# Expert weights laid with consecutive rows in a partition, and the feature order that follows

## The reference: what is computed

```python
def rms_norm(x, g):
    xf = x.astype(jnp.float32)
    y = xf * lax.rsqrt(jnp.mean(xf * xf, axis=-1, keepdims=True) + RMS_EPS)
    return (y * g.astype(jnp.float32)).astype(x.dtype)
...
    x = x + merged @ w_mix_o[l]
    h = rms_norm(x, norm_ffn_g[l])
    x = x + hierarchical_moe(h, ...)          # router: 36 logits a token, 2 of 32 experts chosen
...
def expert_block(args):                       # xb: the rows routed to expert e
    xb, e = args
    hid = jax.nn.silu(xb @ w_gate[e]) * (xb @ w_up[e])     # 1024 -> 512
    return hid @ w_down[e]                                 # 512 -> 1024
```

## Time and profile before

| | |
|---|---|
| time, median of 3 runs | 2509.94 us (2508.97 to 2510.35) |
| span of the profiled execution (first to last instruction) | 2510.5 us |
| TensorE busy | 2324.1 us, 93% |
| VectorE, ScalarE, GpSimd busy | 1099.5, 455.0, 121.8 us |
| bytes moved by DMA | 483.90 MB in 178413 packets |
| mean granted TensorE clock | 0.969 of full |

### The profile page before, as it was taken

The page is one execution under the profiler, slowest core; times in us unless marked ns, Lnnn a source line. Parts: engine busy times, 40 slices in busy tenths (PEclk is TensorE's granted clock), DMA queues, the critical chain, the costliest instruction groups (busy, mean ns, idle before and its releaser), DMA issues. The chain is left out here.

```text
span 2510.5 us, 29002 instructions
## 1 busy us (share of the span) xinstructions
PE 2324.1 (93%) x11012; PEld 1343.9 (54%) x11013; DVE 1099.5 (44%) x1871; ACT 455.0 (18%) x854; POOL 121.8 (5%) x53
## 2 busy tenths in 40 slices
PE   5999999996999999999789999999969999999995
PEld 2448888543455455455344588885435455455453
DVE  6895334324333433433378843434243433433433
ACT  2103333001111111111121223320001111111111
POOL 0002212000000000000000022210000000000000
PEclk9999999998999999999979999999979999999997
DMA  5201101232698898898241011121329898898891
GB/s 191 76 17 51 68 34 68 101 140 101 251 351 329 320 353 325 323 354 325 78 183 42 34 51 51 51 78 74 140 101 335 323 346 333 321 348 330 323 350 42
DMA packets 178413, 483.90 MB, mean 193 GB/s; under 512 B 4128, under 2 KB 4896, under 8 KB 172960
## 3 DMA queue, kind: packets, MB, share of 16 engines
q1 hardware_dynamic: 178336, 482.88, 52.0%
HBM read 476.57 MB, written 6.29 MB: 192 GB/s over the span
## 5 line engine op out<-in xcount | busy, mean ns | idle before, releaser
L754 PEld LDWEIGHTS ps<-arena 128*128 128x128 f32 x2176 | 249.9, 195 | 43.0 <-issue 26.0
L754 PE MATMUL ps<-arena 128*128 128x128 f32 x2176 | 256.4, 280 | 16.4 <-DVE arena L285 16.4
L1612 PE MATMUL ps<-arena 128*64 128x512 f32 x512 | 252.4, 605 | 3.2 <-DVE arena L1357 3.2
L1613 PE MATMUL ps<-arena 128*64 128x512 f32 x512 | 252.4, 605 | 0.0
L1353 DVE TENSOR_TENSOR x_tokens<-x_tokens,ps 128x512 f32<-128x512 f32 x272 | 181.2, 686 | 146.6 <-PE ps L748 145.4
L1612 PE MATMUL ps<-slabs,arena 128*64 128x512 f32 x512 | 225.0, 592 | 0.0
L1613 PE MATMUL ps<-slabs,arena 128*64 128x512 f32 x512 | 224.9, 592 | 0.0
L1346 DVE SCALAR_TENSOR_TENSOR split_rows<-ps,arena,split_rows 64x512 fp32r<-64x512 f32 x128 | 96.0, 750 | 276.4 <-ACT split_rows L957 274.4
L573 PE MATMUL ps<-h_hi,w_parts 128*128 128x512 f32 x768 | 211.6, 411 | 0.0
L428 PE MATMUL ps<-slabs,hT 128*128 128x512 f32 x384 | 174.5, 616 | 9.1 <-DVE hT L1254 7.5
L573 PEld LDWEIGHTS ps<-h_hi,w_parts 128*128 128x128 f32 x768 | 141.5, 194 | 25.7
(11 more groups left out here) (280 smaller groups left out, 3012.3 us busy)
## 6 DMA issues: line engine op xcount, KB each, us to landing
arena<-in_expert_w_gate SPq DMA_DIRECT2D x32, 2048.0 KB, 8.7
arena<-in_expert_w_up SPq DMA_DIRECT2D x32, 2048.0 KB, 13.6
arena<-in_expert_w_down SPq DMA_DIRECT2D x32, 2048.0 KB, 11.1
slabs<-in_expert_w_gate SPq DMA_DIRECT2D x32, 2048.0 KB, 9.7
slabs<-in_expert_w_up SPq DMA_DIRECT2D x32, 2048.0 KB, 14.5
slabs<-in_expert_w_down SPq DMA_DIRECT2D x32, 2048.0 KB, 8.2
slabs<-in_dense SPq DMA_DIRECT2D x18, 2048.0 KB, 8.5
slabs<-in_gate_w SPq DMA_DIRECT2D x24, 1024.0 KB, 4.8
```

What stands on the lines that cost most here:

```text
L754: last = nc.tensor.matmul(ps[:, 2 + d // 4, (d % 4) * P:(d % 4 + 1) * P], xn[:, t, d * P:(d + 1) * P], sel[:, t, :], start=(t == 0), stop= ...
L1612: nc.tensor.matmul(ps[0:64, bank, :], x_k, wg_k, start=(k == 0), stop=(k == ND - 1), tile_position=(0, 0))
L1613: return nc.tensor.matmul(ps[64:P, bank, :], x_k, wu_k, start=(k == 0), stop=(k == ND - 1), tile_position=(0, 64))
```

## The change

The expert weights are laid so that partition `p` takes consecutive rows: rows `8p` to `8p+7` of gate and up, `4p` to `4p+3` of down. A partition's share of a matrix is then one run of 16 KB. Features must lie in the same order in everything that meets these weights:

- `normalise` of the second norm (k = 1) reads x with a step of 8 features and writes `xn` in the order chunk, partition;
- `gffn` and the router's weights `rw` are loaded again in that order, by eight DMAs each of 16 partitions (and one DMA for the router's bias `rb`); the source of the former is single 4-byte elements;
- `hid` is written in the order chunk, partition: the reads stay consecutive, and each written element lies 128 elements (512 bytes) behind the last. 

`w_place` is each slot as a flat run of 4096 elements; the matmuls read it through the same views as before.

```diff
+        w_place = [[view(o, SLAB) for o in w] for w in wslot]
+        def by_rows(a):
+            return a.rearrange("q (c p) -> q p c", c=NH)
+        def in_fours(a):
+            return a.rearrange("q (p c) -> q p c", c=NH)
...
             def expert_rows(ap, e, k):
-                return ap[bass.ds(layer, 1), bass.ds(e, 1)].rearrange("l e (k p) n -> p (l e k) n", p=P, k=k)
+                return ap[bass.ds(layer, 1), bass.ds(e, 1)].rearrange("l e (p k) n -> p (l e k n)", p=P, k=k)
...
                             sp.dma_start(io["x_kept"].rearrange("(t p) d -> p t d", p=P), x).then_inc(s["x_saved"], 16)
+                            sp.wait_ge(s["small_in"], 16)
+                            a0 = SMALL["gffn"][0]
+                            for j in range(ND):
+                                sp.dma_start(small["gffn"][16 * j:16 * j + 16, :],
+                                             row(io["small"])[:, a0 + j].rearrange("(a k) -> a k", k=ND),
+                                             allow_slow_non_contiguous=True).then_inc(s["gffn_in"], 16)
...
-                    sp.dma_start(view(O_KS + N_MCONST, 324), row(io["router"])).then_inc(s["router_in"], 16)
+                    for j in range(ND):
+                        sp.dma_start(rw[16 * j:16 * j + 16], row(io["router"])[:, 36 * j:36 * j + 36].rearrange("(a k) n -> a k n", k=ND))\
+                          .then_inc(s["router_in"], 16)
+                    sp.dma_start(rb, row(io["router"])[:, 288:324]).then_inc(s["router_in"], 16)
...
-                            sp.dma_start(w_gate[b], expert_rows(io["expert_w_gate"], e, ND)).then_inc(w_in_sem[b][0], 16)
+                            sp.dma_start(w_place[b][0], expert_rows(io["expert_w_gate"], e, ND)).then_inc(w_in_sem[b][0], 16)
...
-                    pe.wait_ge(s["router_in"], 16)
+                    pe.wait_ge(s["router_in"], 16 * (ND + 1))
...
-                        tell(v.tensor_scalar(xn[:, t, :], x[:, t, :], rstd[:, one], None, ALU.mult), "xn_ready")
+                        to, of = xn[:, t, :], x[:, t, :]
+                        if k == 1:
+                            to = to.rearrange("q (k p) -> q k p", k=ND)
+                            of = of.rearrange("q (p k) -> q k p", k=ND)
+                        tell(v.tensor_scalar(to, of, rstd[:, one], None, ALU.mult), "xn_ready")
...
                     dve.wait_ge(s["x_back"], 16)
+                    dve.wait_ge(s["gffn_in"], 16 * ND)
...
-                                v.tensor_tensor(hid[0:64], ps[64:P, 0, :], silu[0:64], ALU.mult).then_inc(s["hid_done"], 1)
+                                v.tensor_tensor(by_rows(hid[0:64]), in_fours(ps[64:P, 0, :]), in_fours(silu[0:64]), ALU.mult)\
+                                 .then_inc(s["hid_done"], 1)
```

More of the change, by code:

```diff
@@ L323, in _ @@
                 act.wait_ge(s["pro_act"], 2)
-        names = ("small_in", "bparam_in", "sgu_in", "cglu_in", "router_in", "mconst_in", "slab_in0", "slab_in1", "slab_in2",
+        names = ("small_in", "gffn_in", "bparam_in", "sgu_in", "cglu_in", "router_in", "mconst_in", "slab_in0", "slab_in1", "slab_in2",
                  "chain_dve", "chain_act", "chain_pool", "sumsq_ready", "var_ready", "sd_ready", "xn_ready",
@@ L389, in _ @@
                     sp.wait_ge(s["merge_done"], ND)
-                    load_expert(nc, sp, io, expert_rows, 0, 0, w_gate, w_up, w_down, w_in_sem)
+                    load_expert(nc, sp, io, expert_rows, 0, 0, w_place, w_in_sem)
                     sp.wait_ge(s["outp_done"], ND)
-                    sp.dma_start(view(O_KS + N_MCONST, 324), row(io["router"])).then_inc(s["router_in"], 16)
+                    for j in range(ND):
+                        sp.dma_start(rw[16 * j:16 * j + 16], row(io["router"])[:, 36 * j:36 * j + 36].rearrange("(a k) n -> a k n", k=ND))\
+                          .then_inc(s["router_in"], 16)
+                    sp.dma_start(rb, row(io["router"])[:, 288:324]).then_inc(s["router_in"], 16)
                     sp.dma_start(mc, io["mconsts"]).then_inc(s["mconst_in"], 16)
                     sp.wait_ge(s["proj_done"], J_END - 4)
-                    load_expert(nc, sp, io, expert_rows, 1, 1, w_gate, w_up, w_down, w_in_sem)
+                    load_expert(nc, sp, io, expert_rows, 1, 1, w_place, w_in_sem)
                     with sp.Fori(0, N_EXP // 2 - 1) as i:
@@ L400, in _ @@
                             sp.wait_ge(s["gu_done"], 2 * i + b + 1 + CRED)
-                            sp.dma_start(w_gate[b], expert_rows(io["expert_w_gate"], e, ND)).then_inc(w_in_sem[b][0], 16)
-                            sp.dma_start(w_up[b], expert_rows(io["expert_w_up"], e, ND)).then_inc(w_in_sem[b][1], 16)
+                            sp.dma_start(w_place[b][0], expert_rows(io["expert_w_gate"], e, ND)).then_inc(w_in_sem[b][0], 16)
+                            sp.dma_start(w_place[b][1], expert_rows(io["expert_w_up"], e, ND)).then_inc(w_in_sem[b][1], 16)
                             sp.wait_ge(s["down_done"], 2 * i + b + 1 + CRED)
-                            sp.dma_start(w_down[b], expert_rows(io["expert_w_down"], e, NH)).then_inc(w_in_sem[b][2], 16)
+                            sp.dma_start(w_place[b][2], expert_rows(io["expert_w_down"], e, NH)).then_inc(w_in_sem[b][2], 16)
                 @block.tensor
@@ L1276, in _ @@
                     dve.wait_ge(s["rt_done"], 1)
-                    dve.wait_ge(s["router_in"], 16)
+                    dve.wait_ge(s["router_in"], 16 * (ND + 1))
                     dve.wait_ge(s["mconst_in"], 16)
@@ L1464, in _ @@
                                 def _(sp):
-                                    for w, name, k in ((w_gate, "expert_w_gate", ND), (w_up, "expert_w_up", ND),
-                                                       (w_down, "expert_w_down", NH)):
-                                        sp.dma_start(w[0], expert_rows(io[name], e, k)).then_inc(so["ov_weights"], 16)
+                                    for w, name, k in zip(w_place[0], ("expert_w_gate", "expert_w_up", "expert_w_down"), (ND, ND, NH)):
+                                        sp.dma_start(w, expert_rows(io[name], e, k)).then_inc(so["ov_weights"], 16)
                                     sp.wait_ge(so["ov_weights"], 48)
@@ L1526, in _ @@
                                     dve.wait_ge(so["ov_silu"], 1)
-                                    v.tensor_tensor(hid[0:CAP], ps[64:P, 0, :], silu[0:CAP], ALU.mult).then_inc(so["ov_hid"], 1)
+                                    v.tensor_tensor(by_rows(hid[0:CAP]), in_fours(ps[64:P, 0, :]), in_fours(silu[0:CAP]), ALU.mult)\
+                                     .then_inc(so["ov_hid"], 1)
                                     for n in range(2 * NT):
@@ L1592, in reduce_angle, with load_expert @@
     link(v.tensor_scalar(r2, r2, -1.0, float(np.pi / 2), ALU.mult, ALU.add))
[L1595 to L1598, removed]
+def load_expert(nc, sp, io, expert_rows, e, b, w_place, w_sem):
+    sp.dma_start(w_place[b][0], expert_rows(io["expert_w_gate"], e, ND)).then_inc(w_sem[b][0], 16)
+    sp.dma_start(w_place[b][1], expert_rows(io["expert_w_up"], e, ND)).then_inc(w_sem[b][1], 16)
+    sp.dma_start(w_place[b][2], expert_rows(io["expert_w_down"], e, NH)).then_inc(w_sem[b][2], 16)
 def expert_gather(nc, ps, bank, xn, sel):
```

## The result

| | before | after |
|---|---|---|
| median of 4 runs of each | 2509.45 us (2505.15 to 2510.35) | 2519.85 us (2518.04 to 2521.90) |
| span of the profiled execution | 2510.5 us | 2520.1 us |
| VectorE busy | 1099.5 us | 1126.4 us |
| mean granted TensorE clock of that execution | 0.969 | 0.970 |

The ratio is 1.0046, with a 95% interval of 1.0034 to 1.0057, that is 8.5 to 14.3 us more; the medians differ by 10.4 us and the profiled spans by 9.6 us. The forecast was 7.2 us more. The changed kernel's profiled execution was the slowest of its four (2521.9 us of device time beside a span of 2520.1), so places in the two traces are compared by their lengths, not by their totals.

What follows compares the result with a forecast made beforehand. The prediction took TensorE to bound the kernel, with weights always arriving in time. hid's 6.4 us and the norm's 0.8 gave +7.2 us, loads 0: 2509.9 + 7.2 = 2517.1 us, range 2509.2 to 2524.

Steps and rivals of the forecast that it cites:

- The bound, and the loads: Expert loop: TensorE bounds it, weights always arrive before they are asked for, so larger packets are worth 0 us.
- Rival (d): Expert loads: long runs are slower and loads bound the loop; 15% longer loads give +57 us; chance 0.04.
- (e): Expert loads: 16 KB runs are cut into 2 KB packets, packets stay near 178,000, time as forecast; chance 0.40 together with forecast.
- Rival (c): First products: fewer DMA packets relieve TensorE's reads, 6.7 us come back, 2503.2 us with a free hid; chance 0.05.
- The cover of 0.17 us: Each pair's first expert: spare time per pair before a longer hid on VectorE stops TensorE's transposes.
- rival (a): Stepped write: it is free, or hid grows by less than 0.3 us; 2510 to 2514 us; chance 0.33.
- (b): Each hid element takes two cycles (+11.8 us), norm between 0.8 and 3.2; 2523.2 us; chance 0.18.
- the term of 6.4: hid in the expert loop: 0.37 us longer, 0.17 covered, so 0.20 us per pair, 32 times, 6.4 us.
- The prediction's upper bound: hid's stepped write: one element in two cycles in place of one adds 0.54 us, 11.8 us in all.
- The norm: Each layer's fourth second-norm instruction: its read step costs 0.42 us, 0.8 us in two layers.
- The small loads: gffn's eight and the router's nine DMAs on SyncE: hidden by spare time, all 0 us.
- The baseline: Profiled span of 2510.5 us, taken as 0.6 us above the runs' median; forecast carried to the median from 2509.9.

Runs made afterwards that it cites:

- e1: Kernel before with only the experts' weights laid in 16 KB runs, so the experts' products differ in value: 2508.12 us, 1.000 times before.
- e7: Kernel before with only w_down laid in long runs and hid written with the 512-byte step: 2515.08 us, 1.0024 times before.
- e12: Changed kernel, gffn and router weights reordered in HBM beforehand, hid in two instructions, first two transposes awaiting only the first: 2509.55 us, 1.0000 times before.
- e8: Changed kernel, gffn and router weights reordered in HBM beforehand, hid written consecutively with both inputs read in 16-byte steps: 2517.11 us, 1.0032 times before.
- e11: Kernel before, with half of each layer's last norm computed twice, without a step: 2511.52 us, 1.0008 times before.
- e6: Changed kernel, gffn and router weights reordered in HBM beforehand, w_down and hid as before the change: 2511.32 us, 1.0009 times before.
- e9: Changed kernel, gffn and router weights reordered in HBM beforehand, 49 counting instructions per layer added on SyncE: 2518.15 us, 1.0037 times before.
- e3: Changed kernel with hid written consecutively and its transposes on TensorE reading every fourth element: 2604.22 us, 1.0379 times before.
- e5: The changed kernel measured again, with nothing else altered: 2520.03 us, 1.0040 times before.
- e10: Changed kernel with gffn laid out in HBM beforehand, so only the router's nine small DMAs remain: 2517.92 us, 1.0037 times before.
- e2: Kernel of e1 with hid also written in the 512-byte step; tokens went to other experts: 2859.99 us, 1.1397 times before.

## Why the prediction held, and what it missed

**The bound, and the loads: right.** e1's packets (39072 for 178336) are worth 0 within 2.8 us. Rival (d) falls with the same run, and (e) with 43763 packets, against about 43,750 forecast (8992 under 512 bytes, against 8,990). Rival (c) supposed that many packets slow the first products on `arena`. With a quarter of them the page after has

```profile
L1637 PE MATMUL ps<-arena 128*64 128x512 f32 x512 | 252.3, 605 | 3.2 <-DVE arena L1381 3.2
...
L1638 PE MATMUL ps<-slabs,arena 128*64 128x512 f32 x512 | 224.9, 592 | 0.0
```

the same 605 and 592 ns as the earlier trace rows. The 13 ns have another cause, which stays open.

**hid: right in mechanism and size.** The row taken as nearest, the 16-byte step of line 1315 with 0.73 ns more per element, gave 0.37 us; (1069 - 693)/512 = 0.73 ns and 0.376 us were measured. The cover of 0.17 us came out as 0.376 - 0.20 = 0.18. That excludes rival (a), a free step, and (b), whose 0.54 us more would have made `hid` 1.23 us. e7 puts 6.1 us (3.8 to 8.3) on the term of 6.4, and e12 shows that it is the stall that counts and not VectorE's time. The Trainium skill, "SBUF — State Buffer", section "Door 1: The DMA port swizzle", says that each access to a new 16-byte line pays a penalty; it gives no size for it. e8 and the change agree with it: steps of 16 bytes on the reads and of 512 on the write cost the same, 376 ns for 512 elements. No run here has a step below 16 bytes. The prediction's upper bound, said there to be the sum by this rule, rests on a doubling that is the prediction's own, and the runs show 0.70 of it (376 of 540 ns).

**The norm: right in length, open beyond it.** 0.39 us per layer against 0.42. The prediction scaled line 1585 by 0.52 ns per element; e11 bears that out with 0.49 us for 512 elements beside 0.75 for 1024, 0.51 ns each. What the whole costs, e6 gives only as 2.3 us (0 to 4.5).

**The small loads: this step failed, in part.** "All 0 us" holds for their transfers and their issue. SyncE issues `gffn`'s in 14.04 us and the router's in 5.85 and 8.25 us:

```profile
20.91 14.04 SPq L396 DMA_DIRECT2D arena<-in_small  x8
35.14 1.72 SPq L388 DMA_DIRECT2D slabs<-in_dense  x1
...
529.02 0.33 SPq L1621 DMA_DIRECT2D arena<-in_expert_w_gate  x1
529.45 0.38 SPq L1622 DMA_DIRECT2D arena<-in_expert_w_up  x1
529.92 0.43 SPq L1623 DMA_DIRECT2D arena<-in_expert_w_down  x1
530.53 5.85 SPq L408 DMA_DIRECT2D arena<-in_router  x8
536.57 8.25 SPq L410 DMA_DIRECT2D arena<-in_router  x1
```

Slab 2 is issued at 35.14 and needed at 78, and no engine waits. But I had counted the DMAs and their packets, and not the instructions (some 49, the number that e9 puts in their place) that wait, address and issue in SyncE's loop. They delay SyncE's return in the turn between the layers by some 3.1 to 3.9 us: 12.40 to 13.21 us in the five traces that have such code (after, e3, e5, e9, e10), against 9.26 to 9.40 in the nine without it (before and all others). What TensorE pays is less, because ScalarE is no earlier. Its first product on a slab comes 29.5 to 30.0 us behind the `add_back` in the five and 28.3 to 29.0 in the eight others read for it (all but e2), about 1.1 us more in the mean, and the program's end is some 0.5 us longer (23.3 to 23.6 for 22.8 to 22.9; e1, without the code, has 23.4). So the term put at 0 was 1 to 2 us.

The 9.6 us between the profiled spans are then: 5.9 for the intervals between pairs, 0.8 for the norm, 1.3 for the turn and the end, 0.3 net from stretches at another clock, and 1.3 in stretches in which nobody waits for what was changed. The first three, and 0.4 for the two pairs that lie in other rows of the table, are what the change does: 8.4 us, against 7.2 forecast and an interval of 8.5 to 14.3. The parts measured alone by their medians, 6.1 (e7) and 2.3 (e6), leave the remainder open within their intervals of some 2 us each. Why the median came out at 10.4 and not near 8.4 no run here shows; the interval of e5 (7.0 to 13.0) holds both.

The signs were there: the page counts q14's packets, and the turn of 9.26 us stood in the trace. SyncE shows no work in it; the kernel has it clear the layer's semaphores there, between two barriers of all engines. The Trainium skill, "Runtime: NRT & Kernel Launch", section "Instruction fetch mechanics", has the rule that I should have weighed: instructions are fetched in blocks over a DMA queue of their own, in sequence, and a taken branch to outside the window stalls. The loop over the layers is such a branch. The trace agrees as far as it goes. Between the last `add_back` and SyncE's first DMA, q14 moves 2 packets before (1247 to 1256 us) and 6 after (1251 to 1263.6 us):

```profile
q14 instruction: 2, 0.02, 0.6%
...
q14 instruction: 6, 0.05, 1.1%
```

That SyncE stands still for these packets is inferred; no row shows the wait itself. Why ScalarE too comes back 0.3 us later (0.9 in e9) stays open.

**The baseline.** I set the span of 2510.5 us beside the median of the runs. An execution's own time is 1.8 us above its span (2521.9 and 2520.1), so that profile lay some 2 us above the median, not 0.6. Since only the difference was carried over, the forecast is not touched.

## What to carry to other kernels

Before a transfer is made better, ask who waits for it; here nobody did, and what the new layout asked of the engines was paid wherever TensorE waited for it. When a consumer gets longer by a known amount, read its spare time from the rows before and after it (here 0.17 of 0.37 us) and multiply only the rest, and if the rest hurts, let the reader wait for the first part alone (e12). And count added instructions on the engine that issues a loop's transfers as well as what they do: a longer program delayed that engine by over 3 us at the turn of this loop, though each instruction in it was hidden. Then ask again who waits: of these 3 us TensorE paid about one, because another engine came back as late.

## What the runs showed of the hardware

- **A step on VectorE in fp32** cost 0.73 ns per element for tensor_tensor, whether on one written operand with 512 bytes or on two read ones with 16 bytes (1069 ns for 693). For tensor_scalar a read step of 32 bytes took 1024 elements from 0.75 to 1.14 us, 0.38 ns each.
- **The same step on TensorE's weight load** is paid by the engine that bounds the loop: 327 ns for 191 per load of 128x128 with a step of 16 bytes (e3), and the kernel 3.8% slower.
- **A DMA of single elements** is dear to issue: each of `gffn`'s eight, 128 elements of 4 bytes, holds SyncE for 14.04 / 8 = 1.75 us, where 2 MB of an expert take 0.33 to 0.43 (the first three issues at 529 us).
- **A longer program on SyncE** delayed its first DMA at the turn of the layer loop from 9.3 to between 12.4 and 13.2 us, with DMAs (after, e3, e5, e10) or without them (e9), and TensorE's first product on a slab by about 1.1 us.
- **TensorE's clock in the tail of a layer** differs from run to run. From the last norm to the first `hid`, the kernel before had both lengths in one execution (columns as in the earlier trace rows):

```profile
591.97:644.31 52.34, 33.23 (x146) 18.08 (x146) 23.32 (x62) 3.60 (x7) 0.00 (x0) 0.80 0.31 116
1831.89:1886.11 54.22, 35.34 (x146) 19.02 (x146) 23.38 (x63) 3.60 (x7) 0.00 (x0) 0.75 0.30 112
```

  and the changed one only the longer (in layer 1 it is 54.95 us, also at 0.75):

```profile
592.15:647.11 54.96, 35.47 (x146) 19.03 (x146) 23.70 (x62) 3.60 (x7) 0.00 (x0) 0.75 0.27 111
```

  A mean granted clock of 0.80 over 52.34 us is 21 us at the lower level of 1.2 GHz, 0.75 over 54.96 is 27 us. Over all traces the longer form (54 us and more, against 52.3 to 52.9) came in 2 of 8 layers with the old norm instruction (before, e1, e2, e7) and in 10 of 18 with the new one (e11, with the lengthened norm, 1 of 2). That may be chance. Whether the longer idle time ahead of the transposes makes it more frequent, and so puts more than 0.8 us on the norm, stays open.
